# Inverses of the gated delta rule: full 128x128 levels with masks and transposes, or compact diagonal blocks on small array tiles

## The reference

```python
kb = k * beta[..., None]
A = jnp.where(tri_strict, jnp.einsum('bhncd,bhnsd->bhncs', kb, k) * decay, 0.0)
eye = jnp.eye(C, dtype=jnp.float32)
Tm = lax.linalg.triangular_solve(A + eye, jnp.broadcast_to(eye, A.shape),
                                 left_side=True, lower=True, unit_diagonal=True)
u = jnp.einsum('bhncs,bhnse->bhnce', Tm, v * beta[..., None])
w = jnp.einsum('bhncs,bhnsd->bhncd', Tm, kb * jnp.exp(gc)[..., None])
```

## Time and profile before

| | us |
|---|---|
| median of 3 runs (lowest to highest) | 1255.58 (1255.45 to 1258.73) |
| the profiled execution | 1255.62 |
| its span, first to last instruction | 1253.8 |
| busy: PE | 1240.3 (99%) |
| busy: PEld | 1164.2 (93%) |
| busy: DVE | 918.2 (73%) |
| busy: ACT | 699.1 (56%) |
| busy: POOL | 174.6 (14%) |

### The profile page before, as it was taken

How to read it: one execution, slowest core, us unless ns; L and a number is a source line. 1 busy time by engine, 2 the same in 40 slices (tenths; PEclk the granted TensorE clock), 3 DMA queues, 4 the chain that set the end, 5 groups by cost and what they waited for, 6 DMA issues and landing times.

```text
span 1253.8 us, 23324 instructions
## 1 busy us (share of the span) xinstructions
PE 1240.3 (99%) x9041; PEld 1164.2 (93%) x9041; DVE 918.2 (73%) x1290; ACT 699.1 (56%) x1082; POOL 174.6 (14%) x113
## 2 busy tenths in 40 slices
PE   9999999999999999999999999999999999999998
PEld 8998999999989998889998989999889998999986
DVE  6887864978778774457744548999758777999954
ACT  5556455654456443444345557666547567766652
POOL 0000151000000000000000001664300000466410
PEclk9999999999999999999999999999999999999999
DMA  7553433411456555555553455555565444455562
GB/s 300 182 182 110 154 114 113 156 36 68 172 185 213 174 198 177 192 196 173 194 193 121 148 176 171 191 180 188 206 217 181 154 157 162 169 190 178 193 231 95
DMA packets 30315, 212.84 MB, mean 170 GB/s; under 512 B 3488, under 2 KB 3616, under 8 KB 5152
## 3 DMA queue, kind: packets, MB, share of 16 engines
q1 hardware_dynamic: 29088, 206.53, 47.5%
q0 software_dynamic: 1152, 5.24, 1.3%
HBM read 210.71 MB, written 1.05 MB: 169 GB/s over the span
## 4 chain that ended last, share of the span: by engine, by line
PE 88%; DVE 7%; ACT 3%; issue 1%; DMA 0%; DVEq 0%; POOL 0%; SPq 0%; ACTq 0%; POOLq 0%
PE lin L540 51%; PE lin L702 22%; DVE wlo L513 3%; PE lin L567 2%; PE lin L2887 2%; ACT whi L506 1%; PE lin L569 1%; PE aux L2629 1%; PE aux L2601 1%; PE aux L725 1%; PE aux L2487 1%; ACT lm L1377 1%; PE aux L2557 1%; ACT lm2a L1377 0%; PE aux L2433 0%
## 5 line engine op out<-in xcount | busy, mean ns | idle before, releaser
L513 DVE TENSOR_TENSOR wlo<-raw,whi 128x2048 fp32r<-128x2048 f32 x183 | 422.4, 2311 | 167.0 <-ACT whi L506 166.5
L506 ACT CAST whi<-raw 128x2048 fp32r<-128x2048 f32 x192 | 365.3, 1906 | 175.3 <-DMA raw<-in_stream 143.2
L540 PE MATMUL lin<-xhi,whi 128*128 128x256 f32 (+2 forms) x1616 | 460.2, 285 | 1.0 <-DVE wlo L513 1.0
L540 PE MATMUL lin<-xlo,whi 128*128 128x256 f32 (+2 forms) x1616 | 455.8, 282 | 0.0
L540 PE MATMUL lin<-xhi,wlo 128*128 128x256 f32 (+2 forms) x1616 | 455.7, 282 | 0.0
L540 PEld LDWEIGHTS lin<-xhi,whi 128*128 128x128 f32 x1616 | 305.6, 189 | 2.9 <-DVE wlo L513 1.3
L540 PEld LDWEIGHTS lin<-xhi,wlo 128*128 128x128 f32 x1616 | 305.8, 189 | 0.0
L540 PEld LDWEIGHTS lin<-xlo,whi 128*128 128x128 f32 x1616 | 304.3, 188 | 0.4
L865 POOL TENSOR_TENSOR fu<-fs,ft 128x256 f32<-128x256 f32 x44 | 107.3, 2439 | 259.2 <-ACT fs L1479 259.2
L2294 DVE SCALAR_TENSOR_TENSOR ft<-fy,par,ft 128x254 f32<-128x254 f32 (+1 forms) x176 | 114.8, 691 | 5.9 <-DVE ft L2294 0.2
L540 PE MATMUL lin<-whi,xhi 128*128 128x256 f32 x256 | 73.9, 288 | 0.0
(11 more groups left out here) (454 smaller groups left out, 2137.3 us busy)
## 6 DMA issues: line engine op xcount, KB each, us to landing
raw<-in_stream SPq DMA_DIRECT2D x193, 1024.0 KB, 4.9
gp<-in_gains POOLq DMA_DIRECT2D x6, 512.0 KB, 3.9
c<-in_const SPq DMA_DIRECT2D x1, 1460.0 KB, 16.2
h<-in_x SPq DMA_DIRECT2D x2, 544.0 KB, 4.5
c<-in_const POOLq DMA_DIRECT2D x1, 1024.0 KB, 6.6
ht<-in_xtok POOLq DMA_DIRECT2D x1, 1024.0 KB, 9.9
out<-ht SPq DMA_DIRECT2D x1, 512.0 KB, 2.6
out<-ht SPq DMA_DIRECT2D x2, 256.0 KB, 2.0
```

The costliest lines, as they stand in the source:

```text
L506: nc.scalar.copy(whi[:, s0 % 4], raw[:, s0 % 4]).then_inc(hi_ready, 1)
L513: nc.vector.tensor_tensor(wlo[:, s0 % 4], raw[:, s0 % 4], whi[:, s0 % 4].bitcast(F32), ALU.subtract).then_inc(lo_ready, 1)
L540: ins = nc.tensor.matmul(out, a, b, start=start and n == 0, stop=stop and n == 2)
```

## The change

The inverse is kept as compact diagonal blocks in two forms, `t32` and `n32` (its transpose, made by VectorE's 32x32 turn), eight heads side by side. The level 16 uses four 32x32 tiles on the array's diagonal at once, level 32 two or three tiles, level 64 two 64x64 tiles; the products write the blocks where they belong, so masks, the full transposes and the additions go. GpSimd clears the full matrix `tt` and the 64-row form `n64` and places diagonal blocks in them; VectorE and ScalarE share the evacuations. The weight subtractions of the slots `wbd` 0, 1 and 2 move from VectorE to GpSimd, inside and between its two calls of `inverse`. TensorE's pieces are placed between single input tiles of gate slot 11 and of the `branch` slots, in a new order; the PSUM banks are dealt anew. The masks' constants shrink.

```diff
-NLEVEL = 7
-FIRST_LEVEL = 4
-BLOCK = 1 << FIRST_LEVEL
+BLOCK = 16
...
+        tt = (None, *(at(f"tt{s}", TT[s], [P, 8, P]) for s in (1, 2)))
+        n64 = (None, *(at(f"n64_{s}", TT[s] + 4096, [P, 8, 64]) for s in (1, 2)))
+        t32 = (None, *(at(f"t32_{s}", TT[s] + 6144, [P, 8, 32]) for s in (1, 2)))
+        n32 = (None, *(at(f"n32_{s}", TT[s] + 7168, [P, 8, 32]) for s in (1, 2)))
...
+            def inverse(s, clear_after):
+                pool.wait_ge(S("c16"), s)
+                nc.gpsimd.tensor_copy(xs16[:, :, BLOCK:32], bc(cst("eye32", lo=BLOCK), 8)).then_inc(S("xs16_eye"), 1)
+                clear_after()
+                own.link(nc.gpsimd.memset(tt[s][:], 0.0))
+                nc.gpsimd.memset(n64[s][0:32, :, 32:64], 0.0).then_inc(S("cleared"), 1)
+                pool.wait_ge(S("cleared"), s)
+                low = FIRST["wbd"] + 2 * s - 2
+                pool_low(pool, low, low + 1)
...
+                after(pool, f"n{s}_4")
+                for k in range(2):
+                    r = slice(32 * k, 32 * k + 32)
+                    nc.gpsimd.tensor_copy(n64[s][r, :, r], n32[s][r]).then_inc(S("n64_blocks"), 1)
...
+                after(pool, f"t{s}_4")
+                for k in (2, 3):
+                    r = slice(32 * k, 32 * k + 32)
+                    nc.gpsimd.tensor_copy(tt[s][r, :, r], t32[s][r]).then_inc(S("tt_blocks"), 1)
...
+            inverse(1, spread_read)
+            pool_low(pool, FIRST["wbd"] + 1, FIRST["wbd"] + 2)
+            inverse(2, lambda: pool.wait_ge(S("ke"), 2))
...
+                same = cst("same32").rearrange("p (b i) -> p b i", i=BLOCK).unsqueeze(1).to_broadcast([P, 8, 2, BLOCK])
+                own.link(nc.vector.tensor_tensor(t32[s][:].rearrange("p h (b i) -> p h b i", i=BLOCK), same,
+                                                 y16[:, 0:8].unsqueeze(2).to_broadcast([P, 8, 2, BLOCK]), ALU.mult))
+                nc.vector.transpose(n32[s][:].rearrange("p h i -> p (h i)"), t32[s][:].rearrange("p h i -> p (h i)"))\
+                    .then_inc(S("first_level"), 1)
...
             substitution(1)
             first_level(1)
-            mask(1, 0, 4)
-            mask(1, 1, 4)
-            low_next()
-            low_next()
-            mask_next(1, 4)
-            right(1, 4, 0)
-            right(1, 4, 1)
...
+            products_16(1)
+            joined_16(1)
+            products_32(1)
+            joined_32(1)
+            products_64(1)
+            joined_64(1)
             decayed_queries(1)
...
-            gate_part(11, 0, 4)
-            pe_first_level(pe, 1)
-            gate_part(11, 4, 8)
+            gate_part(11, 0, 1)
+            pe_products_16(pe, 1)
+            gate_part(11, 1, 3)
+            pe_joined_16(pe, 1)
+            gate_part(11, 3, 4)
+            pe_products_32(pe, 1)
+            gate_part(11, 4, 5)
+            pe_joined_32(pe, 1)
+            gate_part(11, 5, 8)
...
+        DIAGONAL = [slice(32 * g, 32 * g + 32) for g in range(4)]
+
+        def pe_products_16(pe, s):
+
+            pe.wait_ge(S("first_level"), s)
+            b = fill(f"x{s}_4")
+            for hh in range(H1):
+                for r in DIAGONAL:
+                    ins = nc.tensor.matmul(b[r, hh * BLOCK:hh * BLOCK + BLOCK], ats[s][r, hh, r], n32[s][r, hh, 0:BLOCK],
+                                           start=True, stop=True)
+            is_full(ins, f"x{s}_4")
...
+                for k in (1, 0):
+                    lo, mid = DIAGONAL[2 * k], DIAGONAL[2 * k + 1]
+                    ins = nc.tensor.matmul(banks[k][lo, w], xs32[mid, hh], t32[s][mid, hh], start=True, stop=True)
...
+                ins = nc.tensor.matmul(b[HALVES[1 - hh % 2], hh // 2 * 64:hh // 2 * 64 + 64], ats[s][0:64, hh, 64:P],
+                                       n64[s][0:64, hh], start=True, stop=True)
...
             corrected(2, 0)
             corrected(2, 1)
-            branch(2, 0, 2)
+            branch(2, 4, 5)
             outputs(2, 0)
             outputs(2, 1)
-            branch(2, 2, 8)
+            branch(2, 5, 8)
             branch(3, 0, 4)
```

More of the change, by code:

```diff
@@ L1283, in act_gdn @@
             branch(0)
-            first_turned(2)
-            for n in range(FIRST_LEVEL, NLEVEL):
-                level(2, n)
+            blocks_joined(2)
+            products_32(2)
+            upper_blocks(2)
+            joined_32(2)
+            products_64(2)
+            joined_64(2)
             nc.scalar.activation(gtmp[:, 2, 0, 1:2], eps[:, 0:1], ACT.Sqrt)
@@ L2053, in dve_gdn @@
             first_level(2)
-            mask(2, 0, 4)
-            mask(2, 1, 4)
+            branch(0)
+            products_16(2)
             residual(2, 0)
+            joined_16(2)
+            products_32(2)
             residual(2, 1)
-            for n in range(FIRST_LEVEL, NLEVEL):
-                if n < NLEVEL - 1:
-                    mask_next(2, n)
-                else:
-                    branch(0)
-                    low_next()
-                right(2, n, 0)
-                right(2, n, 1)
+            joined_32(2)
+            products_64(2)
+            joined_64(2)
+            dve.wait_ge(lo_ready, FIRST["wbd"] + 2)
             low_after(0)
@@ new lines, in pe_joined_16 @@
+        def pe_joined_16(pe, s):
+            after(pe, f"x{s}_4")
+            pe.wait_ge(S("xs16_eye"), s)
+            b = fill(f"n{s}_4")
+            for hh in range(H1):
+                for r in DIAGONAL:
+                    ins = nc.tensor.matmul(b[r, hh * BLOCK:hh * BLOCK + BLOCK], t32[s][r, hh], xs16[r, hh, 0:BLOCK],
+                                           start=True, stop=True)
+            is_full(ins, f"n{s}_4")
+            b = fill(f"t{s}_4")
+            for hh in range(H1):
+                for r in DIAGONAL:
+                    ins = nc.tensor.matmul(b[r, hh * BLOCK:hh * BLOCK + BLOCK], xs16[r, hh], t32[s][r, hh, BLOCK:32],
+                                           start=True, stop=True)
+            is_full(ins, f"t{s}_4")
@@ new lines, in pe_products_32 @@
+        def pe_products_32(pe, s):
+            after(pe, f"n{s}_4")
+            banks = [fill(f"x{s}_5_{k}") for k in range(2)]
+            for hh in range(H1):
+                for k in range(2):
+                    lo, mid = DIAGONAL[2 * k], DIAGONAL[2 * k + 1]
+                    ins = nc.tensor.matmul(banks[k][mid, hh * 32:hh * 32 + 32], ats[s][lo, hh, mid], n32[s][lo, hh],
+                                           start=True, stop=True)
+                    if hh == H1 - 1:
+                        is_full(ins, f"x{s}_5_{k}")
@@ new lines, in pe_joined_32 @@
+        def pe_joined_32(pe, s):
+            after(pe, f"t{s}_4")
+            for k in range(2):
+                after(pe, f"x{s}_5_{k}")
+            banks = [fill(f"y{s}_5_{k}") for k in range(2)]
+            for hh in range(H1):
+                w = slice(hh * 32, hh * 32 + 32)
+                for k in (1, 0):
+                    lo, mid = DIAGONAL[2 * k], DIAGONAL[2 * k + 1]
+                    ins = nc.tensor.matmul(banks[k][lo, w], xs32[mid, hh], t32[s][mid, hh], start=True, stop=True)
+                    if k and hh == H1 - 1:
+                        is_full(ins, f"y{s}_5_1")
+                r = DIAGONAL[1]
+                ins = nc.tensor.matmul(banks[0][r, w], t32[s][r, hh], xs32[r, hh], start=True, stop=True)
+            is_full(ins, f"y{s}_5_0")
@@ L2640, in corrected @@
                     p_ = 4 * g + q
[L2641 removed]
+                    ins = nc.tensor.matmul(b[:, q * P:q * P + P], tt[s][:, p_], vbs[s][:, p_], start=True,
                                            stop=True)
```

287 lines of the change are left out of this document (124 added, 163 removed), and 7 rows, old and new, of the table off.

## The result

The changed kernel takes 1269.91 us (median of 4, 1266.7 to 1271.54), the kernel before beside it 1255.51 us (median of 4): 1.0105 of it, 95% interval 1.0078 to 1.0132. It is slower by 1%, where 1253.7 was forecast and the range ended at 1262. The profiled execution took 1268.84 us, with a span of 1267.0 us: 13.2 us more than the span before.

The account below looks back on a forecast made before the run. TensorE, busy 1240.3 us with 88% of the chain, bounds the kernel. -26.6 - 2.5 + 8.3 + 2.2 + 5.4 + 5.4 = -7.8; with the tail -6.0, with the clock -1.9: 1253.7 us, range 1240 to 1262.

Parts of the forecast that it names:

- Removed work: TensorE in the inverses: 192 product records and 48 transposes go, 26.6 us; idle and seams another 2.5 us.
- the price of tiny rounds: TensorE's small-tile products: rounds of four tiles at 0.04 us, 0.06 for 64 columns; 8.3 us for both problems.
- the text's own mark: Sign in the 32x32 groups: 64 records of `products_16` in 0.6 us; over 0.9 us means rival 2.
- rival 2: Tiny rounds on TensorE each pay their load's latency, 0.11 us: 21 us, not 8.3; 1266 us; chance 0.12.
- its strong form: Small-tile products on TensorE cost 0.059 us for each record: 36 us, total 1281 us; chance 0.02 within rival 2's.
- the changes of shape: TensorE's array mode around the pieces: 0.09 us a change, twelve pieces with two changes each, 2.2 us.
- The lock: GpSimd's weight subtraction holds up VectorE's two-input substitution step, 4.2 us; TensorE stalls 5.4 us in each inverse.
- Rival 1: No lock in the inverses: stalls 2.0 us instead of 10.8, clock costs 1 to 3; 1242.8 us; chance 0.18.
- Tail: Around `outputs(2)`: three `branch` tiles moved ahead, 2.1 us not won behind it; norms' part 0.3 us sooner.
- The clock: Granted clock falls after the two stalls: 2.05 us each, 4.1 us together (2.8 to 6.8).
- the case that decides: Clock falls after the stalls last longer because tiny tiles fill the time after: up to twice the dense 1.7 us.

Follow-up runs that it names:

- spaced: no_lock_aligned with TensorE's pieces spread otherwise among the same dense records and one wait moved; 1242.48 us, 0.9895 of before.
- no_lock: The changed kernel, with GpSimd's three weight subtractions of the stage begun only when VectorE's substitution is over; 1259.35 us.
- before_lock: The kernel before, with only the stage's three weight subtractions moved from VectorE to GpSimd; 1268.79 us, 1.0089 of before.
- filler: aligned, plus 11 unread 256-column matmuls ahead of TensorE's wait for the first blocks in each set; 1257.75 us.
- before_off: The kernel before with 32 bytes of padding behind its constants; 1263.52 us, 1.0066 of before.
- aligned: The changed kernel with 32 bytes of padding behind the constants; 1259.07 us, 1.0023 of before.
- no_lock_aligned: The changed kernel with GpSimd's subtractions begun after the substitutions and 32 bytes of padding behind the constants; 1249.56 us, 0.9956 of before.
- before_64: The kernel before with 64 bytes of padding behind its constants; 1254.20 us, 0.9983 of before.
- probe_lump: before_64 with 256 tiny records in a row ahead of the state's read of set 2; 1260.82 us.
- probe_spread: before_64 with 256 tiny records in four pieces of 64, a dense input tile after each of the first three; 1258.39 us.

## Why the prediction was wrong, step by step

**Removed work, and the price of tiny rounds: right.** 64 records in 16 rounds take 0.66 us at the full clock, 0.11 of it the last one's length: 0.034 us a round, where 0.04 was taken and 0.6 us forecast. In the changed kernel itself the first group lasts 1.0 us (start to start), and by the text's own mark, over 0.9, that would have been rival 2; it is the halved clock, so such a mark has to name the level at which it is read. The seven pieces of a set are 4.5 us in spaced, where 4.2 was put. Rival 2 (0.11 us) is out, and its strong form too. The Trainium skill (TensorEngine Tiling (Array Packing), Instruction Overhead) gives each matmul some 60 cycles; 0.010 us a record over four tiles doesn't agree with each paying that in turn. A dense input tile between two pieces lasts 0.91 us, not 6 x 0.118 = 0.71: 0.20 us a piece for the changes of shape, where 2 x 0.09 was put.

**The lock: right, stalls within 0.5 us.** The first long step (243.95 us in the trace, 243.8 forecast) lasted 4.5 us where 4.2 was put, the second subtraction began 1.4 us into `substitution(2)` as written, and the stalls were 5.2 and 4.9 us where 5.4 each was put. In time the second subtraction came at 293.1 us, not 284: the first long stretch at the low clock lay before it. Rival 1 is out for the kernel as it is, and its waits of 1.2 and 0.8 us are near what no_lock shows (0.9 and 0.7). The Trainium skill (SBUF — State Buffer, Who interferes with whom) has the lock for the whole instruction as a rule; with a step of 4.53 us under a subtraction of 4.61 this trace agrees.

**Tail: right in sum.** The three tiles moved ahead of `outputs(2)` were not won back: 6.55 us late at its end (326.13 against 319.58), 6.05 at the slots behind it. 0.5 us came back, where 0.3 was put.

**The clock: mechanism right, size wrong.** This is the first step that failed. 2.05 us a fall were taken from a 3.4 us fall, with 3.4, twice the 1.7 that such a fall costs, as the upper end. The falls lasted 17.1 and 13.7 us. From the first tiny record to the last of `products_64`, the changed kernel takes 16.2 us in set 1 (252.72 to 268.93); spaced takes 8.4 (248.31 to 256.75) for the same pieces with 12 dense records fewer (1.4 us): 6.4 lost. In set 2, up to `products_64`, it takes 12.4 us (304.79 to 317.20). Spaced takes 10.5 there (287.49 to 297.95), but 1.2 of it are its own stops and 1.6 its own fall (12 dense records in 3.2 us), so 7.7 without them, worked out and not measured: 4.7 lost. That makes 11.1 us instead of 4.1. What was wrong is the bound: the only fall in the trace before lay under dense work, and the text itself named the case that decides, tiny tiles filling the time after the stall, but priced it at twice the dense one instead of at the whole stage's length. before_lock shows the dense case, 3.4 and 6.8 us; the changed kernel, with the same lock and tiny pieces behind it, 17.1 and 13.7. That the pieces alone make this difference is not shown: its stalls were also longer (5.2 and 4.9 us against 3.8 and 3.2), and in no_lock the same pieces with stops of 2.1 and 1.3 us among them had 6.8 us in each set. That the stall starts the fall is what filler's profile and spaced speak for. Luck has a part in the term too: the fall it was taken from comes in some executions and not in others, over the same code. The wait for ScalarE (0.8 us before the 270.00 us record), which I gave nothing, adds up: -7.8 + 11.1 + 0.8 = +4.1, where the stage shows 86.6 - 80.3 (239.52 to 326.13, and 239.28 to 319.58) less 2.15 for the three tiles, +4.2.

**No step at all: the place of the tiles.** This is the second failure, a term put at nothing. The diff's first lines shorten a table, and `HB = PC + 4 * NC1` turns that into 32 bytes for every operand of TensorE. Worth 7.1 us in the profile behind the stage (6.05 late at 349 us, 13.2 at the end), 7.6 in before_off, 10.8 in aligned. By the rows, some 1270 records of 512 columns behind 340 us at 4.1 ns more (233.3 - 229.2 as means) are 5.2 us, and some 4650 of 256 columns at 0.55 ns more 2.6. With the clock at its true size and no move the forecast would have been -1.9 + 7.0 + 0.8, 1261.5 us, just inside the range; the rest is this. Without lock and move the direction flips back: the change as such, in the order of no_lock_aligned, gives 1249.6 us, and in spaced 1242.5, the fastest of all kernels here and 13 us below before. The fair comparison is before_64, whose tiles lie at the same place (1254.2 us): 4.6 us below it, and 11.7.

**What the trace before showed and the prediction didn't use**: instruction supply. The page of before has the packets (q8), and its rows have one for some 128 records. That was enough to ask the question, and I didn't. In the changed kernel it cost nothing that the trace shows; it came up when the lock was out.

## What to carry to other kernels

Before costing a diff's instructions, follow what it does to the sizes in a table of addresses: compare the count of records in equal windows of layers that nobody touched, since busy shares say 100% in both. Before moving a long two-input operation to GpSimd, look for two-input VectorE steps on the critical chain at the time at which it will start; waiting for the chain to end was worth 10 us here. Small tiles on TensorE are cheap per round, but put dense records between groups of 64, and don't let them follow a stall: groups in a row stopped for up to 2.1 us, and behind stalls of 5 us the clock stayed low for up to 17.

## What was not expected of the hardware

- A TensorE record of 512 columns takes 226.8, 228.9 or 233.3 ns by where its tiles start within 128 bytes (0, 64 or 96 bytes from a common origin); one of 256 columns 118.42, 118.10 and 118.65 ns.
- 64 fp32 records on 32x32 tiles with 16 columns last 0.66 us at 2.4 GHz and 0.88 to 0.99 at 1.2 GHz.
- Tiny records at the full clock with little dense work between stop after some 130 to 190 of them, for 0.9 to 2.1 us: in no_lock and no_lock_aligned in both sets, in filler in one of two, in probe_lump. One 16384-byte instruction packet (0.9 to 1.0 us) begins 0.1 to 1.2 us before the last record ahead of the stop, and the next record starts 1.35 to 1.55 us after its end in all six. That the packet brings TensorE's instructions is inferred.
- After stalls of 3.8 and 3.2 us with dense records behind them the granted clock was 0.50 for 3.4 and 6.8 us (before_lock), after stalls of 5.2 and 4.9 us with tiny pieces and single dense input tiles behind them for 17.1 and 13.7 us (after, aligned). Which of the two differences counts, and what ends the long stretch, was not isolated. Tiny pieces without a stop before them kept 1.00 (spaced and filler in set 1, probe_spread).
- With the same code and the same 10.42 of 11.2 us busy before it, the clock fell at about 116 us in seven of thirteen profiled executions, for 3.4 or 6.8 us.
- Executions of aligned and filler, ten each, spread over 10 us (aligned 1254.5 to 1264.9), those of before_64, also ten, over 0.8.
